# Routing of a mixture-of-experts step restated: tile prefix in PSUM, comparisons in parts, indices by one cast; order around the norms changed

## The reference, cut to what matters

```python
def hier_moe(xn, w_rg, b_rg, w_re, b_re, w_gate, w_up, w_down):
    t = xn.reshape(-1, D_MODEL)                                  # 576 x 1024
    g_prob = jax.nn.softmax((t @ w_rg) + b_rg, axis=-1)          # 4 groups
    g_val, g_idx = lax.top_k(g_prob, 1)
    e_logit = ((t @ w_re) + b_re).reshape(-1, 4, 8)              # 32 experts
    sel = jnp.take_along_axis(e_logit, g_idx[:, :, None], axis=1)[:, 0]
    e_val, e_idx = lax.top_k(sel, 2)                             # two experts of that group
    ...
    hid = jax.nn.silu(g) * u * combine[..., None]
    return jnp.einsum('tef,efd->td', hid, w_down)

x += mixer(rmsnorm(x)); x += hier_moe(rmsnorm(x))                # each layer
```

## Time and profile before

| what | value |
|---|---|
| device time, median of 3 runs | 929.25 us (928.39 to 930.89) |
| span of the profiled execution, first to last instruction | 923.8 us |
| busy share of the span | PE 83%, DVE 44%, ACT 28%, POOL 16% |
| DMA | 201.81 MB, mean 218 GB/s |
| mean granted clock of TensorE | 0.916 of full speed |

### The profile page before, as it was taken

One profiled execution on the slowest core, in us unless ns is written; L12 is line 12 of the kernel. 1 busy time (PEld: TensorE's weight loads), 2 busy tenths in 40 slices (PEclk: granted clock), 3 DMA queues, 4 the chain that ended last, 5 costly groups with the idle time before them and its releaser, 6 DMA issues.

```text
span 923.8 us, 12813 instructions
## 1 busy us (share of the span) xinstructions
PE 768.5 (83%) x4895; PEld 481.0 (52%) x4895; DVE 405.7 (44%) x1001; ACT 259.9 (28%) x554; POOL 151.3 (16%) x233
## 2 busy tenths in 40 slices
PE   3899977999899898999733689799999888999730
PEld 2344445868545695555423567544345487555410
DVE  3378695867588370111128677301112162211118
ACT  6020034635111202322213355310014311322113
POOL 1020003000779001332110201000000001333110
PEclk9999996979999889999976899899999979999885
DMA  9462135000532898999869787780131296999946
GB/s 341 145 201 101 51 112 221 2 0 2 200 117 114 290 411 303 409 411 402 351 201 309 198 209 174 212 313 0 49 133 46 70 396 245 405 409 408 396 156 226
DMA packets 75381, 201.81 MB, mean 218 GB/s; under 512 B 14872, under 2 KB 29592, under 8 KB 74264
## 3 DMA queue, kind: packets, MB, share of 16 engines
q1 hardware_dynamic: 58360, 161.77, 48.7%
q0 software_dynamic: 9696, 19.75, 6.1%
q10 hardware_dynamic: 7264, 19.46, 5.8%
HBM read 171.64 MB, written 39.39 MB: 228 GB/s over the span
## 4 chain that ended last, share of the span: by engine, by line
PE 63%; DMA 11%; DVE 11%; ACT 6%; SPq 5%; issue 3%; POOL 0%; PEldq 0%; DVEq 0%; POOLq 0%; PEld 0%; ACTq 0%
PE PSUM L2049 14%; PE PSUM L1852 10%; PE PSUM L1637 8%; PE PSUM L1796 7%; PE PSUM L1873 5%; DMA RING<-in_moe_w_up 3%; PE PSUM L1840 3%; DMA RING<-in_attn_w_qkv 3%; DVE X L1515 2%; SPq L476 2%; PE PSUM L1727 2%; PE PSUM L1999 2%; PE PSUM L1995 2%; DVE XNT L773 2%; PE PSUM L1594 2%
## 5 line engine op out<-in xcount | busy, mean ns | idle before, releaser
L1637 PE MATMUL PSUM<-RING,XNT 128*128 128x512 f32 (+2 forms) x256 | 94.5, 567 | 4.3 <-DMA RING<-in_attn_w_qkv 3.6
L1852 PE MATMUL PSUM<-PH 128*64 128x256 f32 x448 | 85.6, 399 | 8.4 <-DMA PH<-in_moe_w_up 3.9
L671 POOL DMA_INDIRECT PH<-xn_scratch,PH x32 | 32.5, 1017 | 342.4 <-DVEq L1459 247.7
L2049 PE MATMUL PSUM<-PH,XNT 128*128 128x512 f32 (+1 forms) x220 | 88.1, 593 | 0.3 <-PE PSUM L2049 0.3
L1852 PE MATMUL PSUM<-RING,PH 128*64 128x256 f32 x384 | 69.4, 392 | 11.2 <-DMA PH<-in_moe_w_up 6.4
L1594 PE MATMUL PSUM<-ONES,IDENT 128*128 128x128 f32 x348 | 49.8, 314 | 24.1 <-DVEq L1518 23.9
L1490 DVE TENSOR_TENSOR PH<-PH,PSUM 128x128 f32<-128x128 f32 x32 | 9.2, 289 | 136.3 <-ACT PH L976 136.3
L1637 PEld LDWEIGHTS PSUM<-RING,XNT 128*128 128x128 f32 (+1 forms) x256 | 40.4, 177 | 53.9 <-issue 47.7
L1852 PEld LDWEIGHTS PSUM<-PH 128*64 128x64 f32 x448 | 51.6, 144 | 27.0 <-issue 11.9
L1796 PE MATMUL PSUM<-RING,PH 128*128 128x512 f32 (+1 forms) x160 | 62.6, 593 | 0.0
L1594 PEld LDWEIGHTS PSUM<-ONES,IDENT 128*128 128x128 f32 x348 | 48.8, 229 | 24.5 <-DVEq L1518 24.0
(11 more groups left out here) (378 smaller groups left out, 1366.7 us busy)
## 6 DMA issues: line engine op xcount, KB each, us to landing
PH<-in_moe_w_gate SPq DMA_DIRECT2D x28, 512.0 KB, 10.9
PH<-in_moe_w_up SPq DMA_DIRECT2D x28, 512.0 KB, 13.2
RING<-in_moe_w_gate SPq DMA_DIRECT2D x24, 512.0 KB, 11.5
RING<-in_moe_w_up SPq DMA_DIRECT2D x24, 512.0 KB, 16.0
RING<-in_moe_w_down SPq DMA_DIRECT2D x24, 512.0 KB, 16.3
...
```

Source lines behind the costliest of these rows:

```text
L671: pool.indirect_dma_start(out=XG[:, i % 2, :], out_offset=None, in_=xn_d[layer], in_offset=bass.IndirectOffsetOnAxis(ap=IDX[:, i:i + 1], a ...
L1637: last = te.matmul(PSUM[lo:hi, b0 + col // 512, col % 512:col % 512 + n], XT[:, c, t * P:t * P + r], RING[:, c // 2, (c % 2) * QKV + col:( ...
L1852: last = te.matmul(PSUM[m * 64:(m + 1) * 64, 2 + i % 2, 0:2 * FF], XGT[:, i % 2, c, m * 64:(m + 1) * 64], gu[:, :, c, :], start=(c == 0), ...
L2049: last = te.matmul(PSUM[p0:p0 + r, 2 * (i % 2) + w, :], XT[:, c, t * P:t * P + r], slot(SLOT[q])[:, (2 * (c % 3) + w) * 512:(2 * (c % 3) + ...
```

## The change

It restates the routing and moves three things around it.

- The running sum over tiles is made by PE: all-ones matmuls of tile t are accumulated into the columns of all later tiles, so that PSUM holds finished ranks and, in a sixth column block, the totals. Two matmuls become seven.
- On DVE the sums over tiles are gone, overflow is worked out in fewer steps (a table EOFF is made once at the start), two casts are gone, and P1 comes first. R1 is compared in five pieces, one for each tile, with a semaphore for each, and PE multiplies a tile as soon as its piece is there.
- Lists start from a row of the value 8192 (EMPTY), and TOKID holds the token number less 8192, so that the sum is the row to gather and one cast gives IDX. IDXS takes five more matmuls (P1K) and one addition, behind `routed`.
- `keep_busy` runs 18 and 20 matmuls in place of 30 and 24.
- In layer 0's norm and in the GLU `xt_and_store` of tile t - 1 comes ahead of `norm_act` of tile t. A dummy square root loads ACT's table ahead of the norm of the last GLU tile and ahead of the norms behind the experts.
- Not shown: the allocations of the new tiles, and two GLU buffers that move to another place of the same area.

```diff
-            ch(pool.iota(IOI[:, 0:2 * NT], pattern=[[P, NT], [NTOK, 2]], base=1, channel_multiplier=1))
+            ch(pool.iota(IOI[:, 0:2 * NT], pattern=[[P, NT], [0, 2]], base=-int(NONE), channel_multiplier=1))
             ch(pool.tensor_copy(TOKID.rearrange("p t k -> p (t k)"), IOI[:, 0:2 * NT]))
             ch(pool.memset(TOKID[64:P, 4, :], 0.0))
+            ch(pool.memset(EMPTY[:, :], NONE))
...
             for t in range(NT):
-                norm_act(act, 1, t)
                 if t:
                     xt_and_store(act, 0, t - 1)
+                norm_act(act, 1, t)
             xt_and_store(act, 0, NT - 1)
             end_phase(act, 3)
...
+                ch(nc.scalar.activation(TABLE[:, :], EPSC[:, :], ACT.Sqrt))
                 for t in tiles(2 + 2 * layer):
                     norm_act(act, 2 + 2 * layer, t)
...
                     if n:
-                        norm_act(act, 3, t)
                         if t:
                             xt_and_store(act, 1, t - 1)
+                        if t == NT - 1:
+                            ch(nc.scalar.activation(TABLE[:, :], EPSC[:, :], ACT.Sqrt))
+                        norm_act(act, 3, t)
             xt_and_store(act, 1, NT - 1)
...
+            ch(ve.tensor_scalar(EOFF[:, :], E64[:, :], -1.0, float(NE * CAP - CAP), ALU.mult, ALU.add))
...
-                ve.memset(CNT[:, 0, :], 0.0)
                 ve.memset(LG, 0.0)
+                ve.memset(OVS[:, 0:1], 0)
                 ch(ve.memset(GL8, -BIG))
                 dve.wait_ge(S("logits"), layer + 1)
...
 
                 dve.wait_ge(S("ranks"), layer + 1)
-                ps = PSUM[:, 5, 0:2 * NT * 32].rearrange("p (a t n) -> p a t n", a=2, t=NT)
-                for t in range(NT):
-                    ch(ve.tensor_tensor(CNT[:, t + 1, :], CNT[:, t, :], ps[:, 1, t, :], ALU.add))
-                ve.tensor_tensor(RK, CNT[:, 0:NT, :], ps[:, 0], ALU.add)
-                ch(ve.tensor_scalar(OVNI, CNT[:, NT, :], float(CAP - 1), None, ALU.add))
+                ps = PSUM[:, 5, 0:(NT + 1) * 32].rearrange("p (t n) -> p t n", t=NT + 1)
                 ve.memset(OVM, 1.0)
-                ve.tensor_tensor(SLM, RK, bc(E64[:, :].unsqueeze(1), [P, NT, 32]), ALU.add)
-                ch(ve.tensor_scalar(OVNI, OVNI, CAP.bit_length() - 1, None, ALU.logical_shift_right))
-                ch(ve.tensor_scalar(OVN, OVNI, -1.0, 0.0, ALU.add, ALU.max))
-                ch(ve.tensor_tensor_scan(OVI, OVM, OVN, 0.0, ALU.mult, ALU.add))
-                ch(ve.tensor_tensor(OVE, OVI, OVN, ALU.subtract))
-                ch(ve.tensor_scalar(OVB, OVE, float(CAP), float(NE * CAP - CAP), ALU.mult, ALU.add))
-                ch(ve.tensor_tensor(OVB, OVB, E64[:, :], ALU.subtract))
-                ch(ve.scalar_tensor_tensor(out=RK, in0=RK, scalar=float(CAP), in1=bc(OVB.unsqueeze(1), [P, NT, 32]),
+                ch(ve.tensor_scalar(OVNI, ps[:, NT, :], -1.0, 0.0, ALU.add, ALU.max))
+                ve.tensor_tensor(SLM, ps[:, 0:NT], bc(E64[:, :].unsqueeze(1), [P, NT, 32]), ALU.add)
+                ch(ve.tensor_scalar(OVS[:, 1:33], OVNI, CAP.bit_length() - 1, None, ALU.logical_shift_right))
+                ch(ve.tensor_tensor_scan(OVE, OVM, OVS[:, 0:32], 0.0, ALU.mult, ALU.add))
+                ch(ve.scalar_tensor_tensor(out=OVB, in0=OVE, scalar=float(CAP), in1=EOFF[:, :], op0=ALU.mult, op1=ALU.add))
+                ch(ve.scalar_tensor_tensor(out=RK, in0=ps[:, 0:NT], scalar=float(CAP), in1=bc(OVB.unsqueeze(1), [P, NT, 32]),
                                            op0=ALU.is_ge, op1=ALU.mult))
                 ch(ve.tensor_tensor(SLM, SLM, RK, ALU.add))
                 ch(ve.tensor_tensor(ET, EOH, bc(SLM.unsqueeze(2), [P, NT, 2, 32]), ALU.mult))
                 ch(ve.tensor_reduce(SL, ET, AX.X, ALU.add))
                 ch(ve.tensor_copy(SLI, SL))
-                ve.tensor_scalar(SMI, SLI, P - 1, None, ALU.bitwise_and)
-                ch(ve.tensor_scalar(SDI, SLI, P.bit_length() - 1, None, ALU.logical_shift_right))
-                ve.tensor_copy(SMOD, SMI)
-                ch(ve.tensor_copy(SDIV, SDI))
+                ve.tensor_scalar(SDI, SLI, P.bit_length() - 1, None, ALU.logical_shift_right)
+                ch(ve.tensor_scalar(SMI, SLI, P - 1, None, ALU.bitwise_and))
                 if layer == 0:
                     dve.wait_ge(S("rot_out"), 32 * NB)
-                ve.tensor_tensor(R1, bc(IOTA[:, 0:P].unsqueeze(1).unsqueeze(1), [P, NT, 2, P]),
-                                 bc(SMOD.unsqueeze(3), [P, NT, 2, P]), ALU.is_equal)
                 ch(ve.tensor_tensor(P1, bc(IOTA[:, 0:NPAIR].unsqueeze(1).unsqueeze(1), [P, NT, 2, NPAIR]),
-                                    bc(SDIV.unsqueeze(3), [P, NT, 2, NPAIR]), ALU.is_equal))
-                ve.tensor_tensor(P1, P1, bc(TOKID[:, :, :].unsqueeze(3), [P, NT, 2, NPAIR]), ALU.mult
-                                 ).then_inc(S("onehots"), 1)
-
-                dve.wait_ge(S("token_lists"), layer + 1)
-                ps = PSUM[:, 6, 0:NPAIR]
-                ve.tensor_scalar(LSV[:, 0, :], ps, 0.0, NONE, ALU.is_equal, ALU.mult)
-                ch(ve.tensor_scalar(LSV[:, 1, :], ps, float(NTOK) + 0.5, -float(NTOK), ALU.is_ge, ALU.mult))
-                ch(ve.scalar_tensor_tensor(out=LSV[:, 2, :], in0=ps, scalar=-1.0, in1=LSV[:, 0, :], op0=ALU.add, op1=ALU.add))
-                ve.tensor_copy(IDXS, LSV[:, 2, :])
-                ch(ve.tensor_tensor(IDX, LSV[:, 2, :], LSV[:, 1, :], ALU.add))
-                dve.sem_inc(S("routed"), 1)
+                                    bc(SDI.unsqueeze(3), [P, NT, 2, NPAIR]), ALU.is_equal))
+                ch(ve.tensor_tensor(P1T, P1, bc(TOKID[:, :, :].unsqueeze(3), [P, NT, 2, NPAIR]), ALU.mult))
+                for t in range(NT):
+                    ve.tensor_tensor(R1[:, t], bc(IOTA[:, 0:P].unsqueeze(1), [P, 2, P]),
+                                     bc(SMI[:, t].unsqueeze(2), [P, 2, P]), ALU.is_equal).then_inc(S("onehots"), 1)
+                ch(ve.memset(P1[64:P, 4, 1, :], 0.0))
+                ve.tensor_scalar(P1K, P1[:, :, 1, :], float(NTOK), None, ALU.mult).then_inc(S("onehots"), 1)
+                ch(ve.tensor_tensor(OVI, OVE, OVS[:, 1:33], ALU.add))
+
+                dve.wait_ge(S("token_lists"), 2 * layer + 1)
+                ve.tensor_copy(IDX, PSUM[:, 6, 0:NPAIR]).then_inc(S("routed"), 1)
+                dve.wait_ge(S("token_lists"), 2 * layer + 2)
+                dve.wait_ge(S("routed"), layer + 1)
+                ch(ve.tensor_tensor(IDXS, PSUM[:, 5, 0:NPAIR], IDX, ALU.add))
                 for j0 in range(0, 2 * OVP, OVP):
                     eid = EIDT[0:1, 0:OVP * 32].rearrange("p (j n) -> p j n", n=32)
                     ch(ve.tensor_tensor(eid, bc(OVI[0:1, :].unsqueeze(1), [1, OVP, 32]),
@@ -1815,17 +1815,26 @@
                 keep_busy(20, 7)
                 pe.wait_ge(S("chosen"), layer + 1)
 
-                mm = MM.rearrange("p t n -> p (t n)")
-                te.matmul(PSUM[:, 5, 0:NT * 32], UPPER[:, :], mm, start=True, stop=True)
-                last = te.matmul(PSUM[:, 5, NT * 32:2 * NT * 32], ONES[:, :], mm, start=True, stop=True)
+                te.matmul(PSUM[:, 5, 0:NT * 32], UPPER[:, :], MM.rearrange("p t n -> p (t n)"), start=True, stop=False)
+                te.matmul(PSUM[:, 5, NT * 32:(NT + 1) * 32], ONES[:, :], MM[:, 0, :], start=False, stop=False)
+                for t in range(NT):
+                    to = NT if t == 0 else NT + 1
+                    last = te.matmul(PSUM[:, 5, (t + 1) * 32:to * 32].rearrange("p (t n) -> p t n", n=32), ONES[:, :],
+                                     bc(MM[:, t:t + 1, :], [P, to - t - 1, 32]), start=False, stop=(t == NT - 1))
                 last.then_inc(S("ranks"), 1)
-                keep_busy(30, 7)
-                pe.wait_ge(S("onehots"), layer + 1)
-                for i in range(2 * NT):
-                    last = te.matmul(PSUM[:, 6, 0:NPAIR], R1[:, i // 2, i % 2, :], P1[:, i // 2, i % 2, :],
-                                     start=(i == 0), stop=(i == 2 * NT - 1))
+                te.matmul(PSUM[:, 6, 0:NPAIR], ONES[0:1, :], EMPTY[:, :], start=True, stop=False)
+                keep_busy(18, 7)
+                for t in range(NT):
+                    pe.wait_ge(S("onehots"), 6 * layer + t + 1)
+                    for k in range(2):
+                        last = te.matmul(PSUM[:, 6, 0:NPAIR], R1[:, t, k, :], P1T[:, t, k, :],
+                                         start=False, stop=(t == NT - 1 and k == 1))
                 last.then_inc(S("token_lists"), 1)
-                keep_busy(24, 7)
+                pe.wait_ge(S("onehots"), 6 * layer + 6)
+                for t in range(NT):
+                    last = te.matmul(PSUM[:, 5, 0:NPAIR], R1[:, t, 1, :], P1K[:, t, :], start=(t == 0), stop=(t == NT - 1))
+                last.then_inc(S("token_lists"), 1)
+                keep_busy(20, 7)
                 pe.wait_ge(S("routed"), layer + 1)
                 q0 = Q_M[layer]
 
```

(15 more changed lines are left out.)

## The result

The changed kernel takes 918.89 us (median of 4 runs, 915.73 to 920.88); the kernel before, run beside it, 930.07 (928.39 to 935.65). The ratio is 0.989, 95% interval 0.985 to 0.993: faster by some 11 us, 6 to 14 by the interval. Timed twice more, it came to 0.9905 [0.987, 0.994] and 0.987 [0.983, 0.992].

The account below looks back on a forecast made before the run. DMA time lost while SP waits for round 0's gate and up matmuls was taken as the bound; 4.0 (layer 0) + 2.2 (layer 1) + 0.3 (tails) = 6.5 us, from 929.25 to 922.8 us, range 917.2 to 926.5.

Parts of the forecast that it names:

- The bound: Expert phase: ending round 0's gate and up matmuls earlier shortens each layer by no more than its lost DMA time.
- the hole: DMA time lost around round 0 while SP waits for freed slots: 4.4 us in layer 0, 7.8 in layer 1.
- the forecast was 4.0: Layer 0: gain from closing its lost DMA time, at most 4.4 us, 2.8 if only the second window counts.
- about 2 us of the gain over: Layer 0: of the 6.5 us by which `routed` comes earlier, about 2 are spare once the DMA gap closes.
- The steps to `routed`: Routing: rank matmuls 1.65 us, ranks to lists 4.8, to `routed` 7.5; `routed` 6.5 earlier in layer 0, 5.7 in layer 1.
- The rule weighed in the prediction: ACT, layer 1's norm: a table switch costs 2.66 us with drain, making the norm-order term 1.6 us, not 3.0.
- The 0.3 us for the tails: Behind the experts: no table load between square and root, 0.1 us a layer, 0.3 in all at most.
- The forecast of 2.2: Layer 1: PE starts round 0 3.9 us earlier, loses 1.7 to the lower clock; lost DMA time shrinks by 2.2.
- layer 1 loses less: Rival, chance 0.25: full clock gains layer 1 3.9 us, a 4.0 us gather 6.2; kernel at 920.7 to 918.4.
- The gather: First gather of each layer: 7.0 us beside full DMA; a rival, chance 0.04, had it wait for loads ahead, 934.9.
- 5.45 longer by what lies around the span: Whole kernel: the median of the runs exceeds the profiled span by 5.45 us, turning span 917.3 into 922.8.
- the rival that it was to reach, 926.8: Rival, chance 0.10: lost DMA time does not set the phase's end, layer 0 gains nothing, 2.5 us remain.

Follow-up runs that it names:

- early_gather: Changed kernel with gather indices from constants right behind the choice of experts and 4 unused matmuls in place of 20; 0.988 to the kernel before.
- after: The changed kernel, unedited, in its first profile; the profiled execution took 919.63 us.
- before: The kernel without the change, run beside the changed one; median 930.07 us in the first timing.
- after_again: The changed kernel once more, unedited, for a second profile; median 919.65 us.
- after_third: The changed kernel, unedited, for a third profile on another chip; 0.987 to the kernel before, 916.97 us.

## Why the prediction was right

- **The bound held.** In layer 0, sorted by the column "layer 0: round 0", the hole falls from 4.9 us (47.0) over 2.8 (45.0) and 1.2 (43.5) to 0.1 to 0.4 at 42.1 and below, and the weights from 151.5 to some 145.5 (early_gather apart). The weights less the hole are 144.9 to 146.6 us in all runs but that one. Below 42 nothing more comes. Layer 0 gave 4.0 and 4.4 us in the first two pairs; the forecast was 4.0.
- **Nothing was spare in layer 0.** The prediction had about 2 us of the gain over, but 1.2, 0.4 and 0.2 us of the hole are left in the three profiles. Round 0 ended 43.5, 42.1 and 41.8 us behind the first load where it had ended at 47.0 and 46.6: 3 to 5 us earlier, not the 6.5 that were carried over. One reason is the clock: gate and up took 6.55 us in after for 5.36, which the sum had left as they were (5.35 and 5.36 in the other two). The other is the hole's edges: in windows of 1 us of before the share falls from 353 (0.85, 0.55, 0.06), not at 354.5, and reaches 1.03 again only in the window from 360, 2.4 us behind the end of the matmuls at 357.62.
- **The steps to `routed` were right:** ranks 1.70 us (forecast 1.65), 4.85 to the lists (4.8), 7.56 to `routed` (7.5), logits of tile 3 straight behind those of tile 2. In layer 0 the first gather is issued 26.7, 26.5 and 26.5 us behind the last matmul of the output projection, in the two profiles of before 33.1 and 31.5: 4.8 to 6.6 earlier (6.5). In layer 1 `routed` came 5.7 us earlier relative to the GLU, as worked out: 766.17 to 755.05, less the 5.4 by which its last sigmoid was ahead.
- **Table load.** ACT's rows in layer 1:

```profile
730.63 1.28 ACT L1096 ACT_TABLE_LOAD   x1
731.92 0.20 ACT L1096 ACTIVATE TABLE<-EPSC 128x1 f32<-128x1 f32 x1
732.15 1.06 ACT L751 ACTIVATE XNT<-X 64x1024 f32<-64x1024 f32 x1
```

  The root stands 0.01 us behind the load and the square 0.03 behind the root. The rule weighed in the prediction (the Trainium skill, "ScalarE: Activation LUTs", What ACT_TABLE_LOAD costs) has some 1.38 us of drain on top of the load; these rows do not agree with it. Nor do the others: all 322 loads in the 14 profiles take 1.28 us, and behind 168 of them the next activation starts 0.01 us later; in after every other one waits for another engine or a DMA. The 0.3 us for the tails came to nothing that is seen.
- **Layer 1 was mis-sized by the clock.** The forecast of 2.2 was 3.9 earlier at PE, less 1.7 for the lower clock. Relative to the GLU, gate and up began 3.1 us earlier, 0.4 of the difference being a gather of 7.4 for 7.0, and took 6.15 us in place of 3.67 (6.03 in after_again): round 0 gained 0.6, the layer to its last weight 1.7 and 1.4. In after_third, at full clock, it gained 3.0. The hole, of which the forecast was to take 2.2, stayed at about 8 us in these two. What came beside the 0.6 is a stretch behind round 0 that is 1.0 shorter (101.8 for 102.8 and 102.7): 3.5 and 3.6 us of DMA time are lost in it where 4.5 and 4.3 were, most of the difference in its last 12 us. The sum has no term for that, and its cause is open, so that 2.2 lies near 1.7 and 1.4 is partly luck. In after_third the hole shrank to 5.8; that is nearest to the rival "layer 1 loses less".
- **The gather** took 6.9 to 7.5 us (forecast 7.0), and did not wait for all the loads ahead of it. In layer 1 of after its first packet moved 4.31 us behind its issue, when 1.76 MB of weights had gone by; from 760 to 764 us it moved 0.56 MB beside 1.00 MB of weights. The Trainium skill ("DMA: Bandwidth & Descriptors", Queues, rings and completion order) lets the engines go round between queues, which fits a gather that is slowed and not stopped: 4.2 with the loads held, 7.4 beside them. Some 2.5 of these 3.2 us lie ahead of the gather's first packet, and what it waits for there is not shown.
- **The base was off.** "5.45 longer by what lies around the span" failed: about 2.0 us lie around it in every run. The profiled execution of before took about 925.8 us, less than its median; 3.5 us of the term were scatter. On spans the forecast was 917.3, and 917.7, 916.5 and 914.2 were measured. (The range's upper end, 926.5, also falls short of the rival that it was to reach, 926.8.)
- **The rest stays open.** The two layers account for 5.7 and 5.8 us in the first two pairs and for 8.6 in after_third against the mean of before; the timing says 9 to 12 (its intervals begin at 5 to 8). The profiles of before (925.8 and 925.0 us) lie below its medians (927.7 to 933.3), and its longer executions have no trace. The shift is not one of the long executions alone: on the two chips on which both kernels ran again, the shortest span of before is 922.8 and 921.9 us (14 and 11 executions), of the changed kernel 913.3 and 914.2 (10 and 5), and a straight line of span against mean granted clock through all 40 puts the changed kernel 9 us lower at equal clock. So some 2 to 3 us of the gain lie outside these stretches, in executions without a trace, and have no place yet.
